# First mixer's attention: zero-padded keys per head and a later square root, in a float32 two-block model kernel

## What is computed

```python
def fox_attention(q, k, v, log_f):
    ...
    c = jnp.cumsum(log_f, axis=1).transpose(0, 2, 1)
    qh = q.transpose(0, 2, 1, 3) * (dh ** -0.5)
    ...
        logits = jnp.einsum('bhqd,bhkd->bhqk', q_blk, kh).astype(jnp.float32)
        logits = logits + c_blk[..., None] - c[:, :, None, :]
        mask = p_blk[:, None] >= k_pos[None, :]
        logits = jnp.where(mask, logits, -jnp.inf)
        p = jax.nn.softmax(logits, axis=-1)
        return jnp.einsum('bhqk,bhkd->bhqd', p.astype(vh.dtype), vh)
    ...
def rglru(x, ga_w, ga_b, gx_w, gx_b, lam):
    ...
    a = jnp.exp(log_a)
    u = jnp.sqrt(-jnp.expm1(2.0 * log_a)) * (i * xf)
    ...
def even_mixer(hn, w_in, conv_w, conv_b, ga_w, ga_b, gx_w, gx_b, lam, f_b, w_out):
    ...
    return jnp.concatenate([y_a, y_b], axis=-1) @ w_out
```

## Time and profile before

| | us |
|---|---|
| median of 3 runs | 2518.72 |
| lowest, highest | 2518.15, 2520.06 |
| the profiled execution | 2519.74 |
| its span, first to last instruction | 2518.0 |

### The profile page before, as it was taken

The page is one execution under the profiler, slowest core; times in us unless marked ns, Lnnn a source line. Parts: engine busy times, 40 slices in busy tenths (PEclk is TensorE's granted clock), DMA queues, the critical chain, the costliest instruction groups (busy, mean ns, idle before and its releaser), DMA issues.

```text
span 2518.0 us, 39541 instructions
## 1 busy us (share of the span) xinstructions
PE 2463.0 (98%) x14290; PEld 2101.2 (83%) x14290; DVE 2033.7 (81%) x2944; ACT 1534.1 (61%) x2127; POOL 71.7 (3%) x157
## 2 busy tenths in 40 slices
PE   9999999899999999999999999999999999999998
PEld 8788887788888888888888878889888888898887
DVE  6777764699899989998999977789877877798776
ACT  5554453577777877777777754463644644644543
POOL 9000000000000000000000000000000000000000
PEclk9999999999999999999999999999999999999999
DMA  7456643499999999999999966643566566533663
GB/s 208 127 175 185 185 143 114 145 368 369 357 359 366 375 352 356 374 361 360 357 375 366 362 205 187 193 117 105 161 193 189 169 192 186 149 102 109 197 194 101
DMA packets 481899, 597.30 MB, mean 237 GB/s; under 512 B 21883, under 2 KB 313155, under 8 KB 481761
## 3 DMA queue, kind: packets, MB, share of 16 engines
q1 hardware_dynamic: 478048, 589.47, 69.9%
q0 software_dynamic: 3712, 6.00, 0.8%
HBM read 594.35 MB, written 1.05 MB: 236 GB/s over the span
## 4 chain that ended last, share of the span: by engine, by line
PE 86%; DVE 7%; ACT 2%; issue 2%; DMA 2%; POOL 1%; ACTq 0%; DVEq 0%; POOLq 0%
PE bank L820 22%; PE bank L626 16%; PE bank L662 12%; PE bank L846 11%; PE bank L632 8%; PE bank L611 5%; PE bank L608 2%; DVE wlo_ring L2098 2%; DMA raw_ring<-in_od_exp_w_dram 2%; PE bank L1452 1%; PE bank L1150 1%; PE bank L831 1%; ACT whi_ring L1502 1%; PE bank L882 1%; PE bank L988 1%
## 5 line engine op out<-in xcount | busy, mean ns | idle before, releaser
L2098 DVE TENSOR_TENSOR wlo_ring<-raw_ring,whi_ring 128x1024 fp32r<-128x1024 f32 (+1 forms) x1122 | 1329.4, 1220 | 119.1 <-ACT whi_ring L1502 102.7
L1502 ACT CAST whi_ring<-raw_ring 128x1024 fp32r<-128x1024 f32 (+1 forms) x1122 | 1143.6, 1052 | 166.5 <-DMA raw_ring<-in_od_exp_w_dram 153.5
L626 PE MATMUL bank<-x,whi_ring 128*128 128x512 f32 x1720 | 428.3, 391 | 0.0
L626 PEld LDWEIGHTS bank<-x,whi_ring 128*128 128x128 f32 x1720 | 315.5, 188 | 60.7
L632 PEld LDWEIGHTS bank<-x,wlo_ring 128*128 128x128 f32 x1720 | 220.9, 191 | 8.4
L632 PE MATMUL bank<-x,wlo_ring 128*128 128x256 f32 x1720 | 223.5, 283 | 0.0
L1566 ACT COPY arena<-bank 128x256 f32<-128x256 f32 x110 | 40.9, 372 | 283.9 <-PE bank L632 283.9
L611 PE MATMUL bank<-x,whi_ring 128*128 128x256 f32 (+2 forms) x1024 | 192.8, 289 | 1.2 <-DVE x L2168 0.9
L820 PE MATMUL bank<-whi_ring,xg0hi 128*128 128x512 f32 x448 | 177.7, 397 | 0.3 <-issue 0.3
L820 PE MATMUL bank<-whi_ring,xg1hi 128*128 128x512 f32 x448 | 177.2, 395 | 0.0
L820 PE MATMUL bank<-whi_ring,xg0lo 128*128 128x512 f32 x448 | 174.8, 390 | 0.0
(11 more groups left out here) (518 smaller groups left out, 3435.5 us busy)
## 6 DMA issues: line engine op xcount, KB each, us to landing
raw_ring<-in_od_exp_w_dram SPq DMA_DIRECT2D x672, 512.0 KB, 5.5
raw_ring<-in_ffn_w_gate_dram SPq DMA_DIRECT2D x88, 512.0 KB, 4.0
raw_ring<-in_ffn_w_up_dram SPq DMA_DIRECT2D x88, 512.0 KB, 5.0
raw_ring<-in_ffn_w_down_dram SPq DMA_DIRECT2D x88, 512.0 KB, 3.5
raw_ring<-in_ev_ffn_w_dram SPq DMA_DIRECT2D x66, 512.0 KB, 3.9
raw_ring<-in_w_in_dram SPq DMA_DIRECT2D x42, 512.0 KB, 4.1
raw_ring<-in_od_w_in_dram SPq DMA_DIRECT2D x24, 512.0 KB, 3.8
raw_ring<-in_ev_w_in_dram SPq DMA_DIRECT2D x20, 512.0 KB, 6.8
```

Source lines behind the costliest of these rows:

```text
L626: mm_ = mm(bank[:, :], wh[:, kt, :], X2[:, kt, :, :].rearrange("p a n -> p (a n)"), start=(start and kt == 0), stop=(stop and kt == KT - 1 ...
L1502: nc.scalar.copy(WHI[:, slot, 0:n], RAW[:, slot, 0:n]).then_inc(s["hi_ready"], 1)
L2098: V_.tensor_tensor(WLO[:, slot, 0:n], RAW[:, slot, 0:n], WHI[:, slot, 0:n].bitcast(F32), ALU.subtract)\
```

## The change

`K`, four tiles of 128 x 256, becomes `KZ`, eight tiles, one per head, with the head's 64 channels on their own partitions and zeros on the other 64. POOL writes the zeros; ACT evicts keys in two halves of 64 partitions (`evict_keys`). Scores then use `Q` and `KZ` of all 128 partitions. Values take both heads' 128 channels of `V` as one operand and write 128 partitions, of which the head's 64 are read later; `PVB` therefore holds twice the columns, and ACT's and DVE's splits are made in two halves each (`hi_heads`, `lo_heads`). `SEL2` and `LFP` are filled at two offsets and not at four, which takes away two POOL selects and one DVE operation. `SELR` is cast after the eviction of u(5). The square root moves behind `exps(0)`, `exps(1)`, the keys' eviction and `ahead`. Two of DVE's splits move to a later step: `lo(3)` from v = 8 to 9, `lo(5)` from v = 10 to 11.

```diff
--- before.py
+++ after.py
@@ -255,7 +255,7 @@
-        YR, Q, K = c(4, S), c(4, S), c(4, S)
+        YR, Q, KZ = c(4, S), c(4, S), c(8, S)
...
@@ -270,7 +270,7 @@
-        PVB = (BANK[6][:, 0:S], BANK[7][:, 0:S], BANK[0][:, 0:S], BANK[0][:, S:2 * S])
+        PVB = (BANK[6], BANK[7], BANK[0], BANK[0])
...
@@ -489,9 +489,10 @@
+            link(nc.gpsimd.memset(KZ[:, :, :], 0.0))
...
-            for o in (0, 32, 64, 96):
+            for o in (0, 32):
...
@@ -994,11 +995,11 @@
                 def scores(v):
...
-                    o, n = 64 * (h % 2), (t + 1) * P
+                    n = (t + 1) * P
...
-                    mm(BANK[2 + v % 2][:, 0:S], SELR[o:o + 64, h, :], NCTR[o:o + 64, :], start=True, stop=False, skip_group_check=True)
-                    mm(BANK[2 + v % 2][:, 0:n], Q[o:o + 64, h // 2, t * P:(t + 1) * P], K[o:o + 64, h // 2, 0:n],
+                    mm(BANK[2 + v % 2][:, 0:S], SELR[:, h, :], NCTR[:, :], start=True, stop=False, skip_group_check=True)
+                    mm(BANK[2 + v % 2][:, 0:n], Q[:, h // 2, t * P:(t + 1) * P], KZ[:, h, 0:n],
...
                 def turn_probs(v):
@@ -1012,12 +1013,12 @@
                 def values(v):
...
-                    o = 64 * (h % 2)
+                    o = S * (h % 2) + t * P
...
                     if v == 12:
...
-                        last = mm(PVB[h // 2][o:o + 64, t * P:(t + 1) * P], V[:, b, h * 64:(h + 1) * 64],
+                        last = mm(PVB[h // 2][:, o:o + P], V[:, b, h // 2 * P:(h // 2 + 1) * P],
...
@@ -1727,6 +1728,14 @@
+                def evict_keys(u):
+
+                    act.wait_ge(s["chunk_used"], c0 + u + 4)
+                    act.wait_ge(s["bank_free"], q0 + u)
+                    for x in range(2):
+                        last = af(KZ[64 * x:64 * x + 64, u - 11 + x, :], BANK[(q0 + u) % 2][64 * x:64 * x + 64, 0:S], ACT.Copy)
+                    last.then_inc(s["bank_free"], 1)
@@ -1754,17 +1763,22 @@
                 ahead(c0 + 14)
-                evict(11, K[:, 0, :], ACT.Copy)
+                evict_keys(11)
...
                 ahead(c0 + 15)
...
                 ahead(c0 + 16)
-                act.wait_ge(s["root_in"], 1)
-                af(TH[:, :, :], TH[:, :, :], ACT.Sqrt).then_inc(s["root_ready"], 1)
...
                 def hi(kt, src):
...
+
+                def hi_heads(p):
+                    act.wait_ge(s["pv_ready"], 4 * p + 4)
+                    for x in range(2):
+                        rows = slice(64 * x, 64 * x + 64)
+                        last = nc.scalar.copy(XHI[rows, 4 + p, :], PVB[p][rows, x * S:(x + 1) * S])
+                    last.then_inc(s["evhi_ready"], 1)
...
                 def copy(v):
...
@@ -1783,8 +1797,10 @@
                 exps(0)
                 exps(1)
-                evict(13, K[:, 1, :], ACT.Copy)
+                evict_keys(13)
                 ahead(c0 + 17)
+                act.wait_ge(s["root_in"], 1)
+                af(TH[:, :, :], TH[:, :, :], ACT.Sqrt).then_inc(s["root_ready"], 1)
                 for v in range(16):
                     if v < 8 and v % 2:
                         ahead(c0 + 17 + v // 2)
@@ -1792,15 +1808,14 @@
-                            evict(u, K[:, u // 2 - 5, :], ACT.Copy)
+                            evict_keys(u)
                     if v == 7:
...
                     if v == 12:
-                        act.wait_ge(s["pv_ready"], 12)
-                        hi(6, PVB[2])
+                        hi_heads(2)
                     if v == 7:
...
                     if v + 2 < 16:
@@ -1813,15 +1828,13 @@
                     if v == 9:
                         ahead(oc + 1)
                     if v == 10:
-                        act.wait_ge(s["pv_ready"], 8)
-                        hi(4, PVB[0])
-                        hi(5, PVB[1])
+                        hi_heads(0)
+                        hi_heads(1)
                         ahead(oc + 2)
                     if v in (13, 14, 15):
                         ahead(oc + v - 10)
                 ahead(oc + 6)
-                act.wait_ge(s["pv_ready"], 16)
-                hi(7, PVB[3])
+                hi_heads(3)
                 ahead(oc + 7)
...
@@ -2441,8 +2454,6 @@
-                dve.wait_ge(s["consts_ready"], 1)
-                V_.tensor_copy(SELR[:, :, :], SEL2[:, :, :])
...
@@ -2454,12 +2465,14 @@
-                    last = V_.tensor_scalar(LFP[:, t, :].rearrange("p (o z) -> p o z", o=4)[:, :, 0:8],
+                    last = V_.tensor_scalar(LFP[:, t, :].rearrange("p (o z) -> p o z", o=4)[:, 0:2, 0:8],
...
-                                            .broadcast_to([P, 4, 8]), -1.0, None, ALU.mult)
+                                            .broadcast_to([P, 2, 8]), -1.0, None, ALU.mult)
...
+                dve.wait_ge(s["consts_ready"], 1)
+                V_.tensor_copy(SELR[:, :, :], SEL2[:, :, :])
                 dve.wait_ge(s["bank_free"], q0 + 6)
...
@@ -2477,9 +2490,8 @@
                 dve.wait_ge(s["conv_ready"], 1)
                 dve.wait_ge(s["cum_ready"], 1)
...
-                for o in (32, 96):
-                    V_.scalar_tensor_tensor(NCTR[o:o + 8, :], BANK[2][o:o + 8, 0:S], -1.0, NCTR[o:o + 8, :].bitcast(F32),
-                                            ALU.mult, ALU.subtract)
+                V_.scalar_tensor_tensor(NCTR[32:40, :], BANK[2][32:40, 0:S], -1.0, NCTR[32:40, :].bitcast(F32),
+                                        ALU.mult, ALU.subtract)
...
                 dve.wait_ge(s["cumev_ready"], 1)
@@ -2522,6 +2534,14 @@
                     dve.wait_ge(s["evhi_ready"], kt + 1)
...
+
+                def lo_heads(p):
+                    dve.wait_ge(s["evhi_ready"], 4 + p + 1)
+                    for x in range(2):
+                        rows = slice(64 * x, 64 * x + 64)
+                        last = V_.tensor_tensor(XLO[rows, 4 + p, :], PVB[p][rows, x * S:(x + 1) * S],
+                                                XHI[rows, 4 + p, :].bitcast(F32), ALU.subtract)
+                    last.then_inc(s["x_ready"], 1)
...
@@ -2549,21 +2569,22 @@
                     if v == 7:
...
                     if v == 8:
-                        for kt in (2, 3):
-                            lo(kt, YR[:, kt, :])
+                        lo(2, YR[:, 2, :])
                         ahead(oc)
                     if v == 9:
+                        lo(3, YR[:, 3, :])
                         ahead(oc + 1)
                     if v == 10:
-                        lo(4, PVB[0])
-                        lo(5, PVB[1])
+                        lo_heads(0)
                         ahead(oc + 2)
+                    if v == 11:
+                        lo_heads(1)
                     if v == 12:
-                        lo(6, PVB[2])
+                        lo_heads(2)
                     if v in (13, 14, 15):
                         ahead(oc + v - 10)
                 ahead(oc + 6)
-                lo(7, PVB[3])
+                lo_heads(3)
                 ahead(oc + 7)
                 dve.wait_ge(s["x_ready"], 16)
```

## The result

| | kernel before | changed kernel |
|---|---|---|
| median of 19 runs each, us | 2517.89 | 2523.80 |
| ratio, 95% interval | | 1.0022 (1.0016 to 1.0028) |
| profiled execution, us (span) | 2519.74 (2518.0) | 2522.58 (2520.9) |
| TensorE begins what follows the mixer at, us | 129.71 | 135.85 |

What follows compares the result with a forecast made beforehand. TensorE bounds the program (98% of the span), alternating in the attention with DVE and ACT chains. Step 12 +2.9 (start's gain included), tail -2.15, clock +1.7 make +2.45: median 2521.2 us, range 2515.5 to 2525.5.

Steps and rivals of the forecast that it cites:

- The shapes' price: In the attention, 49 changes of array shape on TensorE cost 0.18 us each; removing them saves at most 8.8 us.
- Rival C: In the attention, the 0.18 us belongs to the sequence of short matmuls, not the shape; +4.6 us, 2523.3, chance 0.12.
- Start: Ahead of the attention, shorter POOL and DVE work removes two TensorE waits, and nothing new waits on POOL; -1.2 us.
- The root: On ACT ahead of step 2: the moved square root leaves step 2's exponential 0.4 to 0.8 us earlier.
- The second split at step 11: TensorE waits at step 12 for lo_heads(1), late in DVE's queue: +4.15 less 1.25, +2.9 us; some 5 us idle.
- After it: From step 12 to the mixer's end, TensorE has 12 shape changes fewer; -2.15 us.
- the clock: Behind step 12's idle time TensorE's clock falls to half pace for 3.4 us of matmuls; +1.7 us.
- the mixer's end: A sign of being right: the mixer's last matmul comes 1 to 4 us later than 129.9.
- step 0's transposes: At the attention's first step, a sign of being right: these transposes come near 68 us, some 3 us earlier.
- Rival A: The wait at step 12 does not grow and TensorE stays warm; -2.2 us, 2516.5, chance 0.15.
- Rival B: The clock falls several times, in steps 2 to 5, 8 and 12; +5.85 us, 2524.6, chance 0.13.
- Any difference after the mixer: A sign of being wrong: what follows the mixer was forecast to be untouched; no size given.

Runs made afterwards that it cites:

- e1: The changed kernel with lo_heads(1) back in step 10, ahead of the cast's remainder; ratio to the kernel before 1.0018, mixer's end 134.93 us.
- e6: The kernel before with only its second remainder, lo(5), moved from step 10 to step 11; ratio 1.0024, mixer's end 138.10 us.
- e2: The changed kernel with 24 matmuls that compute nothing in TensorE's wait at step 12; ratio to the kernel before 1.0020, mixer's end 134.17 us.
- e7: The changed kernel with root before the exponentials, TensorE's mask wait at the mixer's end, first two pairs split one or two steps earlier; ratio to the kernel before 0.9994.
- e4: The changed kernel with TensorE's wait for the second mask flag moved to the mixer's end; ratio to the kernel before 1.0017, mixer's end 135.61 us.
- e5: The kernel before with only the whole-array form, its halves and shorter constants; root, selector cast and remainders unmoved; ratio 1.0007, mixer's end 134.54 us.
- e9: e7 with 19 matmuls that compute nothing at step 0 and 15 at step 8; ratio to the kernel before 1.0003, mixer's end 130.82 us.
- e12: e7 with 10 matmuls that compute nothing at step 0 and 7 at step 8; ratio to the kernel before 0.9991, mixer's end 129.11 us.
- e10: e8 with 11 matmuls that compute nothing at step 0; ratio to the kernel before 0.9989, mixer's end 129.21 us.
- e11: e8 with 6 matmuls that compute nothing at step 0; ratio to the kernel before 0.9984, mixer's end 128.11 us.
- e8: The kernel before with the selector cast behind the eviction of u(5) and TensorE's mask wait at the mixer's end; ratio 0.9994, mixer's end 129.66 us.
- e3: The changed kernel with the square root ahead of the first two exponentials again; ratio to the kernel before 1.0018, mixer's end 134.10 us.

## Why the prediction was right in kind and short in size

- **The shapes' price, 0.18 each and 8.8 in all: right, somewhat high.** 7.2 measured. That the gain is lost where TensorE waits for DVE and ACT was said for steps 3 to 7; it held for all that lies ahead of step 12. Rival C, that the price is not the shape's, falls, although its time of 2523.3 is the nearest of all to the median: the gaps are gone and the work is 7.2 less. Values that load 128 columns cost nothing that can be seen.
- **Start, -1.2: the step failed.** TensorE's two waits went, and at 51 us it was 1.0 ahead (the gates' first matmul, 51.11 against 52.12). But "nothing new waits on it", said of POOL, was wrong. I had followed POOL's queue to the selector and not to its end, where a flag stands that TensorE waits for. The waiting 1.24 us turned the gain into scores 0.25 later.
- **The root: the step that came out with the wrong sign.** Step 2's exponential, forecast 0.4 to 0.8 earlier (the start's 1.2 included), came at 74.62, 1.18 later. What the root feeds, DVE's product, was forecast 1.5 earlier and came at 76.40, 0.23 later. ACT's own rows account for it. From the end of the last cast (67.01 before, 66.66 after) to that exponential it is 6.43 us before and 7.96 after. Of the 1.53 more, 1.10 is the wait for logits, which the root used to cover, less 0.39 of the old wait; 0.5 is the eviction of keys in halves (forecast 0.27), and the rest some tenths in exponentials and cast. I had added up ACT's instructions, without asking what their old place had hidden.
- **The second split at step 11: right in mechanism and place.** The idle time was 5.92 where some 5 was forecast (4.5 to 5.5 among the signs), ended by L2542, with all of TensorE's queue behind it. The step-12 term was +2.9, and measured +5.73. Of the 2.83 between them, 2.16 come from the two steps above (ACT's copies at 106.44 and not 105.53 - 1.25 = 104.28). The rest is 5.96 us from there to the end of `lo_heads(1)`, where the sum had 5.30: the four copies took 1.50 instead of the 1.17 that I had added up, and DVE's chain between the two remainders was a few tenths longer. e1 and e6 show the place in the queue by itself: 3.3 to 3.5.
- **After it, -2.15, and the clock, +1.7.** The tail became 0.41 longer, against -0.45 forecast. By e2 the clock's share is +2.45, so without it the tail is 2.04 shorter, which is the -2.15. The clock's term was short by 0.75, for it stayed down through the wait and some 5 us of matmuls behind it, not 3.4.
- **Together**: 2.83 + 0.75 + 0.11 = 3.7, which is 6.14 less the 2.45 forecast. So the forecast was right on which wait grows and that the kernel gets slower, and it gave 40% of the size. Two of its own signs failed besides: the mixer's end was to come 1 to 4 us later and came 6.14 later, and step 0's transposes, foretold near 68, came at 70.05. That 2523.80 still lies in the range is owed in part to its width of 10 us.
- **Rival A** (no larger wait at step 12) did not happen. It needed `lo_heads(1)` out of step 11; e7 shows it, with 0.26 us there. **Rival B**'s several falls did not occur in the changed kernel's profiled execution, but did in e4 and e5. Its time of 2524.6 is nearer to the median than the forecast's. Whether some unprofiled executions had more than one fall was not seen, but it would fit: the mean granted clock over the span was 0.994 in the profiled execution, 0.993 in the one of 2523.80 us and 0.991 in the slowest, 2527.64.
- **"Any difference after the mixer" would prove it wrong.** The spans did differ there by 3.2 us, from falls of the clock at other places between 410 and 490 us and at 1460 us. The medians differ by about as much as the mixer's ends (5.9 and 6.1), which leaves no sign of a difference behind the mixer over many executions, as far as one trace of each can say.

## What to carry to other kernels

Work taken off an engine shortens a program only up to the next engine's round: before a saving of 7 us on TensorE is counted, ask at each step who releases it, and when a remainder or a split is moved by a step, count everything that stands ahead of it in its new queue. An instruction may be where it is because it fills a wait; moved behind the wait, it stands bare on the chain, as the root did with its two table loads, at a cost of 1.4 to 2.5 us. And if an engine is made to start earlier, follow every flag that it waits for to the end of the queue that sets it; where idle time of two microseconds or so is left, filling it is worth a trial, to its length and no further. In e9 to e12 the clock stayed up at each filled place, and where the filling outlasted the wait (e9, e10) the end came 1.7 and 1.1 us later than with the shorter one (e12, e11).

## What the hardware showed that I had not expected

- **POOL's time depends on what DVE does.** The same four selects took 1.03 us before and 2.81 after, and TensorE's wait for POOL was 1.24, 2.53, 0.73 and 2.80 in four kernels that differ nowhere before it. The section "SBUF: two separate sides" of the Trainium skill's "SBUF — State Buffer" says that a DVE operation with two inputs in SBUF and a GpSimd operation that reads SBUF exclude each other for a whole instruction; the trace agrees so far as the long selects are those with DVE's two-input operations beside them (e4).
- **Half the partitions is not half the time.** A copy of 64 x 256 out of the array's results took 0.375 us on ACT (1.50 for four), where 128 x 256 took 0.31 in the earlier trace rows; DVE's remainder took 0.43 against 0.38. Splitting by partitions more than doubles the cost.
- **Short idle times did not always cost the clock.** 1.67 us at step 0 left it up in the kernel before, and 1.68 took it down in e6 and e8. 2.27 or 2.28 at step 8 left it up in the changed kernel, e1 and e3, and took it down in e2, e4 and e5. 2.01 us at step 11 took it down in e7 and e9, and 2.03 left it up in e12. 2.47 us and more at step 12 took it down each time, but elsewhere such waits did not always: 2.75 at step 0 left it up in e7, and 2.80 ahead of the scores in e3, where 2.73 and 2.53 at the same places took it down in e5 and e1. So the length of a wait alone does not decide it. Section "Part 1" of the Trainium skill's "TensorE: Matmul & The Clock Gate" sets the clock by how busy TensorE has been recently, and the rows at 0.50 agree in that each low stretch begins in or behind idle time; which of the short waits will do it could not be told from these traces.
- **Left open.** A variant with e12's edits and the kernel before's array shape at step 0 only, or with the long waits of steps 4, 5 and 11 removed, wasn't tried. So whether the 7.2 us can be had at all, by giving ACT and DVE less to do in each round, stays open.
